# Gated delta rule on one NeuronCore: making the raw k kᵀ and k qᵀ products once per chunk pair and keeping them for both directions

## The chip, the core and the metric

The kernel runs on one NeuronCore of a Trainium2 chip. The metric is the device time of one execution in microseconds. Shown are three runs of the kernel before and one further execution recorded by the hardware profiler.

## What is computed

Two transformer blocks of width 1024 over 512 tokens, in fp32. The change lies in the first block, in its bidirectional gated delta rule: 8 heads of dimension 128, run once in increasing and once in decreasing position. The part of the reference that matters:

```python
def gated_delta_rule(q, k, v, g, beta):
    ...
    g = jnp.cumsum(g, axis=-1)
    decay = jnp.exp(jnp.where(tri_incl, g[..., :, None] - g[..., None, :], -jnp.inf))
    k_beta = k * beta[..., None]
    lower = jnp.where(tri_strict, jnp.einsum('bhncd,bhnsd->bhncs', k_beta, k) * decay, 0.0)
    rhs = jnp.concatenate([v * beta[..., None], k_beta * jnp.exp(g)[..., None]], axis=-1)
    sol = lax.linalg.triangular_solve(lower, rhs, left_side=True, lower=True, unit_diagonal=True)
    u, w = sol[..., :dv], sol[..., dv:]
    qk = jnp.einsum('bhncd,bhnsd->bhncs', q, k) * decay
    def step(state, xs):
        qd, kt, ui, wi, qki, gl = xs
        v_new = ui - jnp.einsum('bhck,bhkv->bhcv', wi, state)
        o = jnp.einsum('bhck,bhkv->bhcv', qd, state) + jnp.einsum('bhcs,bhsv->bhcv', qki, v_new)
        state = state * jnp.exp(gl)[..., None, None] + jnp.einsum('bhck,bhcv->bhkv', kt, v_new)
        return state, o

o_fwd = gated_delta_rule(q, k, v, g[:, :, 0], beta[:, :, 0])
o_bwd = rev(gated_delta_rule(rev(q), rev(k), rev(v), rev(g[:, :, 1]), rev(beta[:, :, 1])))
```

The products k kᵀ (the gram) and k qᵀ hold neither decay nor beta: these come in afterwards, element by element, and are what differs between the directions.

## The kernel before, in words

**Rounds.** The kernel cuts the 512 tokens into NC = 4 chunks of 128. The delta rule runs in eight rounds R = 0 to 7; `half = R // 4` picks four heads, `r = R % 4` the step of the scan. A round holds J = 8 problems: the four heads in the forward direction on chunk r (j = 0 to 3) and the same heads in the backward direction on chunk 3 − r (j = 4 to 7). So rounds r and 3 − r of a half use the same two chunks, with the directions exchanged. All of it lies in `delta(R)`, which each engine has for itself; semaphores join the four.

**The head of a round**, in the order of its data:
- TensorE (PE) spreads the cumulated decays into pA (L918), makes the eight grams k kᵀ into pB (L925, semaphore `gram`), runs a piece of a filler, waits for `eg` and makes the eight k qᵀ into pA (L933, semaphore `kq`), then runs a second piece of filler.
- VectorE (DVE) subtracts decays from pA into `et` (L2108), derives `en` (L2113) and masks `et` (L2117). ScalarE (ACT) takes the exponents: `qd` from pA (L1504, semaphore `eg`), `en` (L1506), `et` (L1508).
- DVE multiplies the grams in pB by beta and by `en`, eight instructions of 128x128 (L2124, semaphore `L`). ACT copies the diagonal blocks to `lc` (L1515, L1516). GpSimd (POOL) masks `lc` for each of six levels into `ls` (L2528). PE starts level 0 from the first `ls` (L902).
- DVE makes `tb` (L2133) and `ub` (L2135) from level 0; PE needs `ub` for level 1. At levels 1 and 2 DVE multiplies k qᵀ, still in pA, by `et`, 128x512 at a time (L2157).

**Fillers.** Between the steps of a round PE runs dense products of 128x512 (L641) of other projections, cut by the tables `GAP` and `GAP3`: in rounds 0 to 5 there are 14 products between L925 and L933 and 14 more before level 0, in rounds 6 and 7 there are 16 and 17. Each product has a weight tile that ACT (w_hi, L1210) and DVE (w_lo, L1788) have split. DVE has filler of its own, the taps of a 31-wide convolution (L1868), placed by the table `TAP`: three of them come between L2124 and L2133 in rounds 0 to 4, then more at each level. In round 7 the filler of PE is the product of the convolution's result; it waits for each slice k of `a_lo`, of which POOL makes slices 0 to 5 (L2561) and DVE slices 6 and 7 (L1847), in its order behind L2124.

The order on each engine is that of the program text; nothing is moved by a scheduler.

```python
dve.wait_ge(S("gram"), R + 1)
dve.wait_ge(S("en"), R + 1)
...
ins = dve.scalar_tensor_tensor(en[:, j], pB[:, j], scal(6, j), en[:, j], ALU.mult, ALU.mult)
...
if R == 7:
    for t in range(6, KT):
        low("conv", t, cslot(t))
```

Of the kernel before, what the change touches and what calls it, by code (L numbers as in the profile page):

```python
# [17 lines left out]
ALU = mybir.AluOpType  # L18
# [101 lines left out]
def build(nc, a, out):  # L120

    ctx = ExitStack()
    with ctx:
# [23 lines left out]
        w_lo = at("w_lo", 2 * UC, F32R, shape=[P, 2, UC])  # L147
        A_OFF = base[0]
# [43 lines left out]
        J = 2 * HH  # L192
        en = at("en", J * P, shape=[P, J, P])
# [429 lines left out]
        def _(pe):  # L623
# [282 lines left out]
            def delta(R):  # L906
# [15 lines left out]
                for j, d, hh, c in prob:  # L922

                    tok = slice(c * P, (c + 1) * P)
                    ins = pe.matmul(pB[:, j, :], kT[:, hh, tok], kT[:, hh, tok], start=True, stop=True)  # L925
                ins.then_inc(S("gram"), 1)
# [3 lines left out]
                pe.wait_ge(S("eg"), R + 1)  # L930
                for j, d, hh, c in prob:
                    tok = slice(c * P, (c + 1) * P)
                    ins = pe.matmul(pA[:, j, :], kT[:, hh, tok], qT[:, hh, tok], start=True, stop=True)  # L933
                ins.then_inc(S("kq"), 1)
                gap(R, 1)
                for lv in range(LEVELS):

                    pe.wait_ge(S("ls"), LEVELS * R + lv + 1)
                    if lv == 0:
# [4 lines left out]
                        if R == 5:  # L944

                            pe.wait_ge(S("csum"), KT - 1)
                            pe.matmul(nb, ones, acc[:], start=True, stop=True).then_inc(S("mean"), 1)
# [18 lines left out]
                    pe.wait_ge(S("ycp"), LEVELS * R + lv)  # L966
                    wait(pe, "t_upd", (LEVELS - 1) * R + lv - 1)
# [235 lines left out]
        def _(act):  # L1203
# [63 lines left out]
            def high_o(h):  # L1267
                act.wait_ge(S("on_z" if h < HH else "on_g"), h + 1)
                if h < HH:
                    act.wait_ge(S("kq"), 8)  # L1270
                    act.wait_ge(S("qdm"), 8)
                act.activation(o_hi[:, h], oT[:, h], ACT.Copy).then_inc(S("a_hi"), 1)
# [215 lines left out]
            def delta(R):  # L1488
# [27 lines left out]
                act.activation(lc[hi_], en[hi_, :, hi_], ACT.Copy).then_inc(S("lc"), 1)  # L1516
                gap(R, 0)
                gap(R, 1)
# [264 lines left out]
        def _(dve):  # L1783
# [309 lines left out]
            def delta(R):  # L2093
# [26 lines left out]
                dve.wait_ge(S("gram"), R + 1)  # L2120
                dve.wait_ge(S("en"), R + 1)
                dve.wait_ge(S("kf"), 3 * (half + 1))
                for j in range(J):
                    ins = dve.scalar_tensor_tensor(en[:, j], pB[:, j], scal(6, j), en[:, j], ALU.mult, ALU.mult)  # L2124
                ins.then_inc(S("L"), 1)
                if R == 7:
# [9 lines left out]
                for lv in range(1, LEVELS):  # L2136
# [15 lines left out]
                    if lv in (1, 2):  # L2152

                        dve.wait_ge(S("kq"), R + 1)
# [517 lines left out]
```

## Time and profile before

| | |
|---|---|
| three runs | 2248.22, 2248.62, 2251.39 us; median 2248.62 us |
| profiled execution, own time | 2249.63 us |
| its span in the trace | 2247.8 us |
| PE busy | 2181.4 us, 97% of the span |
| VectorE / ScalarE / GpSimd busy | 1274.1 us (57%) / 820.4 us (36%) / 196.0 us (9%) |
| chain that ended last | PE 80%, issue 10%, VectorE 7%, ScalarE 2% |

The delta rounds lie from about 217 to 430 us (R = 0 to 3) and from 530 to 752 us (R = 4 to 7). A PE matmul's end is modelled in the profile, so that neighbouring matmuls overlap by a little: what a group of matmuls takes from PE is read from its start to the start of what follows. An fp32 matmul of the program is two rows in the trace (x16 for eight). A number in square brackets is the time that the engine idled before the row, and for whom.

### The profile page before, as it was taken

The page shows a single profiled execution, that of the slowest core. Times are in us where ns is not written, and L with a number is a line of the kernel's source. Part 1 is how long each engine was busy: PE and PEld are TensorE (multiplying, and loading weights), DVE is VectorE, ACT ScalarE, POOL GpSimd, SP SyncE. Part 2 cuts the span into 40 slices and gives each one's busy share as a digit, 9 for nine tenths or more (in the row PEclk, how much of TensorE's full clock was granted, in tenths as well). Part 3 has the DMA queues.
Part 4 walks back from the last instruction along what each step waited for, and adds up shares of the span by engine and source line. Part 5 has one row for each costly group of instructions (what it writes and reads, how often), then busy time and mean ns, then how long its engine had stood idle before and what let it go on. Part 6 is the DMA issues. An engine that isn't in the chain of part 4 may idle for free.

```text
span 2247.8 us, 34856 instructions
## 1 busy us (share of the span) xinstructions
PE 2181.4 (97%) x14232; PEld 1819.0 (81%) x14232; DVE 1274.1 (57%) x1889; ACT 820.4 (36%) x1256; POOL 196.0 (9%) x142
## 2 busy tenths in 40 slices
PE   7999999998999999999999999999999899999998
PEld 5878788787888888888888888888897588888887
DVE  4789999887765555444532554443237736444423
ACT  4344434345444233232222532322233534232222
POOL 0100222102333001000000100000000110000000
PEclk9999999999999999999999989999999889999999
DMA  4232111121111243332332323333321112322321
GB/s 160 78 131 78 56 44 44 57 72 57 35 49 63 99 140 118 102 94 93 114 103 66 120 66 97 99 93 112 102 67 57 38 57 67 102 94 93 116 96 51
DMA packets 56171, 189.88 MB, mean 84 GB/s; under 512 B 6257, under 2 KB 8689, under 8 KB 56049
## 3 DMA queue, kind: packets, MB, share of 16 engines
q1 hardware_dynamic: 53168, 182.88, 25.3%
q10 hardware_dynamic: 2880, 5.24, 0.6%
q8 instruction: 92, 1.51, 0.3%
q14 instruction: 31, 0.25, 0.0%
HBM read 178.66 MB, written 9.44 MB: 84 GB/s over the span
## 4 chain that ended last, share of the span: by engine, by line
PE 80%; issue 10%; DVE 7%; ACT 2%; POOL 0%; DMA 0%; SPq 0%; ACTq 0%; DVEq 0%; POOLq 0%
PE pg L641 68%; PE pC L902 4%; PE pB L902 1%; DVE cpad L1868 1%; DVE w_lo L1788 1%; DVE sacc L2009 1%; PE pB L672 1%; ACT w_hi L1210 1%; PE pA L962 1%; PE pC L745 1%; PE pA L719 0%; PE pB L679 0%; PE pB L703 0%; PE pC L719 0%; PE pC L1170 0%
## 5 line engine op out<-in xcount | busy, mean ns | idle before, releaser
L641 PE MATMUL pg<-a_hi,w_hi 128*128 128x512 f32 (+1 forms) x1920 | 748.9, 390 | 12.4 <-DVE a_lo L1847 3.4
L641 PE MATMUL pg<-a_lo,w_hi 128*128 128x512 f32 (+1 forms) x1920 | 741.1, 386 | 0.0
L641 PE MATMUL pg<-a_hi,w_lo 128*128 128x512 f32 (+1 forms) x1920 | 738.6, 385 | 0.0
L1788 DVE TENSOR_TENSOR w_lo<-w_raw,w_hi 128x1024 fp32r<-128x1024 f32 (+3 forms) x299 | 382.6, 1279 | 399.2 <-ACT w_hi L1210 396.8
L1210 ACT ACTIVATE w_hi<-w_raw 128x1024 fp32r<-128x1024 f32 (+3 forms) x299 | 329.6, 1102 | 651.7 <-PE pg L641 640.7
L641 PEld LDWEIGHTS pg<-a_hi,w_hi 128*128 128x128 f32 x1920 | 364.0, 190 | 87.6 <-issue 8.0
L641 PEld LDWEIGHTS pg<-a_hi,w_lo 128*128 128x128 f32 x1920 | 363.6, 189 | 69.1 <-issue 1.6
L641 PEld LDWEIGHTS pg<-a_lo,w_hi 128*128 128x128 f32 x1920 | 363.8, 190 | 68.0 <-issue 0.9
L641 PE MATMUL pg<-h_hi,w_hi 128*128 128x512 f32 (+1 forms) x572 | 215.7, 377 | 0.6 <-DVE w_lo L1788 0.6
L641 PE MATMUL pg<-h_hi,w_lo 128*128 128x512 f32 (+1 forms) x572 | 214.5, 375 | 0.0
L641 PE MATMUL pg<-h_lo,w_hi 128*128 128x512 f32 (+1 forms) x572 | 212.4, 371 | 0.0
L2274 DVE TENSOR_TENSOR tmp<-pg,rstd 128x512 f32<-128x512 f32 x66 | 45.6, 691 | 188.6 <-PE pg L641 188.6
L1868 DVE SCALAR_TENSOR_TENSOR cpad<-cpad,vec 128x512 f32<-128x512 f32 x180 | 144.0, 857 | 0.3
L641 PEld LDWEIGHTS pg<-h_hi,w_lo 128*128 128x128 f32 x572 | 107.4, 188 | 21.3
L641 PEld LDWEIGHTS pg<-h_lo,w_hi 128*128 128x128 f32 x572 | 107.3, 188 | 20.4
L641 PEld LDWEIGHTS pg<-h_hi,w_hi 128*128 128x128 f32 x572 | 107.5, 188 | 19.2 <-DVE w_lo L1788 1.0
L2528 POOL TENSOR_TENSOR ls<-lc,consts 128x512 f32<-128x512 f32 x48 | 74.2, 1557 | 467.8 <-ACT lc L1516 422.1
L2575 POOL TENSOR_TENSOR acc<-acc,sq 128x512 f32<-128x512 f32 x22 | 29.7, 1349 | 819.3 <-ACT sq L1253 819.3
L1597 ACT ACTIVATE h_hi<-tmp 128x512 f32 (+1 forms) x66 | 41.7, 632 | 131.7 <-DVE tmp L2278 131.7
L2516 POOL TENSOR_TENSOR acc<-acc,sq 128x512 f32<-128x512 f32 x22 | 30.5, 1388 | 570.8 <-ACT sq L1227 570.5
L2283 DVE TENSOR_TENSOR h_lo<-tmp,h_hi 128x512 f32 (+1 forms) x66 | 45.7, 693 | 58.3 <-ACT h_hi L1597 58.3
L2269 DVE TENSOR_TENSOR tmp<-pg,rstd 128x512 f32<-128x512 f32 x66 | 45.6, 691 | 55.0 <-PE pg L641 54.9
(361 smaller groups left out, 2376.4 us busy)
## 6 DMA issues: line engine op xcount, KB each, us to landing
w_raw<-in_w_gu SPq DMA_DIRECT2D x132, 512.0 KB, 3.5
w_raw<-in_w_in SPq DMA_DIRECT2D x74, 512.0 KB, 3.5
w_raw<-in_w_dn SPq DMA_DIRECT2D x48, 704.0 KB, 4.1
spill_g<-tmp ACTq DMA_DIRECT2D x16, 256.0 KB, 2.1
w_raw<-in_w_co SPq DMA_DIRECT2D x8, 512.0 KB, 3.6
w_raw<-in_w_do SPq DMA_DIRECT2D x8, 512.0 KB, 3.6
w_raw<-in_w_wo SPq DMA_DIRECT2D x8, 512.0 KB, 4.1
w_raw<-in_w_pg SPq DMA_DIRECT2D x8, 512.0 KB, 3.5
```

The source lines that it names most:

```text
L641: ins = pe.matmul(dst[:, cols], w_of(w, n % 2, k), b(k)[:, cols], start=first and q == 0, stop=last and q == len(todo) - 1)
L902: ins = pe.matmul(dst[s, j, :], lhs[s, j, :], id64[s, :] if rhs is None else rhs[s, j, :], start=True, stop=True)
L1210: act.activation(w_hi[:, n % 2, 0:c], w_raw[:, n % 4, 0:c], ACT.Copy).then_inc(S("w_hi"), 1)
L1597: act.activation(h_hi[:, m] if isinstance(i, int) else h_hi[:, bass.ds(m, 1)].rearrange("p a n -> p (a n)"), tmp2[:], ACT.Copy).then_inc(S ...
L1788: dve.tensor_tensor(w_lo[:, n % 2, 0:c], w_raw[:, n % 4, 0:c], w_hi[:, n % 2, 0:c].bitcast(F32), ALU.subtract).then_inc(S("w_lo"), 1)
L1868: ins = dve.scalar_tensor_tensor(y, src, w, y, ALU.mult, ALU.add)
L2269: dve.tensor_tensor(tmp1[:], bg, rstd[:], ALU.mult).then_inc(S("evD"), 1)
L2274: dve.tensor_tensor(tmp2[:], bu, rstd[:], ALU.mult).then_inc(S("evD"), 1)
L2283: dve.tensor_tensor(at_m(h_lo), tmp2[:], at_m(h_hi).bitcast(F32), ALU.subtract)\
L2516: pool.tensor_tensor(acc[:], acc[:], sq[:, t % 2, :], ALU.add).then_inc(S("add"), 1)
L2528: pool.tensor_tensor(ls[:, lv % 2].rearrange("p (d h) c -> p d h c", d=2), lc[:].rearrange("p (d h) c -> p d h c", d=2), mask, ALU.mult)\
L2575: pool.tensor_tensor(acc[:], acc[:], sq[:, t % 2, :], ALU.add).then_inc(S("add"), 1)
```

## The change

The raw grams are made in rounds 0, 1, 4 and 5 only, and the raw k qᵀ in rounds 0, 1, 4, 5 and 6. Behind `lc`, ACT copies the grams of these four rounds, and the k qᵀ of rounds 0, 1 and 4, out of PSUM, as two instructions of 128x512 each (14 in all). They go into columns of the weight buffers that no weight of 1024 columns fills, and for round 1 into two unused tiles of oT. In rounds 2, 3, 6 and 7 DVE reads the gram from the copy of the twin round (3 − r), directions exchanged. In rounds 2, 3 and 7 it also reads k qᵀ there, and multiplies it right behind the grams' eight instructions rather than at levels 1 and 2. In round 5 a single matmul for a mean (into pB) moves from level 0 to level 1, behind ACT's `yb` copy. The diff, cut to its core:

```diff
+        spare = at("spare", 8 * UC, offset=first, shape=[P, 8, UC])
+        GRAM, KQ = (0, 1, 4, 5), (0, 1, 4, 5, 6)
+        def kept(what, R, d):
+            half, r = divmod(R, NC)
+            i = 4 * r + 2 * what + d
+            if i < 4:
+                return spare[:, 2 * i:2 * i + 2, KT * P:KT * P + 2 * P].rearrange("p a (b c) -> p a b c", c=P)
+            if i < 6:
+                s = 4 * (i - 4)
+                return spare[:, s:s + 4, KT * P + 2 * P:UC].rearrange("p (a b) c -> p a b c", b=2)
+            return oT[:, HH + i - 6].rearrange("p (a b c) -> p a b c", b=2, c=P)
+        def twin(R):
+            return R + NC - 1 - 2 * (R % NC)
+        def rounds(which, R):
+            return sum(z <= R for z in which)
 # PE, delta(R)
-                for j, d, hh, c in prob:
-                    tok = slice(c * P, (c + 1) * P)
-                    ins = pe.matmul(pB[:, j, :], kT[:, hh, tok], kT[:, hh, tok], start=True, stop=True)
-                ins.then_inc(S("gram"), 1)
+                if R in GRAM:
+                    for j, d, hh, c in prob:
+                        tok = slice(c * P, (c + 1) * P)
+                        ins = pe.matmul(pB[:, j, :], kT[:, hh, tok], kT[:, hh, tok], start=True, stop=True)
+                    ins.then_inc(S("gram"), 1)
                 gap(R, 0)
-                pe.wait_ge(S("eg"), R + 1)
-                for j, d, hh, c in prob:
-                    tok = slice(c * P, (c + 1) * P)
-                    ins = pe.matmul(pA[:, j, :], kT[:, hh, tok], qT[:, hh, tok], start=True, stop=True)
-                ins.then_inc(S("kq"), 1)
+                if R in KQ:
+                    pe.wait_ge(S("eg"), R + 1)
+                    for j, d, hh, c in prob:
+                        tok = slice(c * P, (c + 1) * P)
+                        ins = pe.matmul(pA[:, j, :], kT[:, hh, tok], qT[:, hh, tok], start=True, stop=True)
+                    ins.then_inc(S("kq"), 1)
-                        if R == 5:
-                            pe.wait_ge(S("csum"), KT - 1)
-                            pe.matmul(nb, ones, acc[:], start=True, stop=True).then_inc(S("mean"), 1)
                     pe.wait_ge(S("ycp"), LEVELS * R + lv)
+                    if R == 5 and lv == 1:
+                        pe.wait_ge(S("csum"), KT - 1)
+                        pe.matmul(nb, ones, acc[:], start=True, stop=True).then_inc(S("mean"), 1)
 # ACT, delta(R)
                 act.activation(lc[hi_], en[hi_, :, hi_], ACT.Copy).then_inc(S("lc"), 1)
+                if r < 2:
+                    for d in range(2):
+                        act.activation(kept(0, R, d), quarter(pB[:, d * HH:d * HH + HH]), ACT.Copy)
                 gap(R, 0)
+                if r < 2 and twin(R) not in KQ:
+                    act.wait_ge(S("kq"), rounds(KQ, R))
+                    for d in range(2):
+                        act.activation(kept(1, R, d), quarter(pA[:, d * HH:d * HH + HH]), ACT.Copy)
 # DVE, delta(R)
-                dve.wait_ge(S("gram"), R + 1)
+                dve.wait_ge(S("gram"), rounds(GRAM, R))
                 for j in range(J):
-                    ins = dve.scalar_tensor_tensor(en[:, j], pB[:, j], scal(6, j), en[:, j], ALU.mult, ALU.mult)
+                    d, hh = divmod(j, HH)
+                    g = pB[:, j] if R in GRAM else kept(0, twin(R), 1 - d)[:, hh // 2, hh % 2]
+                    ins = dve.scalar_tensor_tensor(en[:, j], g, scal(6, j), en[:, j], ALU.mult, ALU.mult)
                 ins.then_inc(S("L"), 1)
+                if R not in KQ:
+                    dve.wait_ge(S("et"), R + 1)
+                    for d in range(2):
+                        z = quarter(et[:, d * HH:d * HH + HH])
+                        dve.tensor_tensor(z, kept(1, twin(R), 1 - d), z, ALU.mult).then_inc(S("qk"), 1)
-                    if lv in (1, 2):
-                        dve.wait_ge(S("kq"), R + 1)
+                    if lv in (1, 2) and R in KQ:
+                        dve.wait_ge(S("kq"), rounds(KQ, R))
```

How it moves instructions, at three places. PE at the head of round 2, before (L1012 ends round 1; the L641 rows are the first filler products):

```order
L1012 MATMUL pC<-bv,kt 128x128 x8
L918 MATMUL pA<-consts,gat 128x128 x8
L925 MATMUL pB<-kT 128x128 x8
L641 MATMUL pg<-a_hi,w_hi 128x512
L641 MATMUL pg<-a_lo,w_hi 128x512
L641 MATMUL pg<-a_hi,w_lo 128x512
```

and now:

```order
L1039 MATMUL pC<-bv,kt 128x128 x8
L943 MATMUL pA<-consts,gat 128x128 x8
L666 MATMUL pg<-a_hi,w_hi 128x512
L666 MATMUL pg<-a_lo,w_hi 128x512
L666 MATMUL pg<-a_hi,w_lo 128x512
```

The filler now follows the decay spread directly; 14 products later the eight k qᵀ matmuls are gone too, so that 28 products stand in a row before level 0.

DVE at the head of round 2, before:

```order
L2193 SCALAR_TENSOR_TENSOR st<-st,gat,pC 128x128 x8
L1788 TENSOR_TENSOR w_lo<-w_raw,w_hi 128x1024
L2108 TENSOR_TENSOR et<-pA,gat 128x512 x2
L2113 TENSOR_SCALAR en<-et 128x1024
L2117 SCALAR_TENSOR_TENSOR et<-et,consts 128x512 x2
L2124 SCALAR_TENSOR_TENSOR en<-pB,gat,en 128x128 x8
L1868 SCALAR_TENSOR_TENSOR cpad<-cpad,vec 128x512 x3
L2133 TENSOR_TENSOR tb<-consts,ls 128x512
L2135 TENSOR_TENSOR ub<-consts,pC 128x512
```

and now (in round 2 the kept k qᵀ lies in oT, in round 3 in spare):

```order
L2234 SCALAR_TENSOR_TENSOR st<-st,gat,pC 128x128 x8
L1822 TENSOR_TENSOR w_lo<-w_raw,w_hi 128x1024
L2142 TENSOR_TENSOR et<-pA,gat 128x512 x2
L2147 TENSOR_SCALAR en<-et 128x1024
L2151 SCALAR_TENSOR_TENSOR et<-et,consts 128x512 x2
L2160 SCALAR_TENSOR_TENSOR en<-spare,gat,en 128x128 x8
L2166 TENSOR_TENSOR et<-oT,et 128x512 x2
L1902 SCALAR_TENSOR_TENSOR cpad<-cpad,vec 128x512 x3
L2174 TENSOR_TENSOR tb<-consts,ls 128x512
L2176 TENSOR_TENSOR ub<-consts,pC 128x512
```

Two multiplications of 128x512 now stand ahead of the three taps and of `tb`; they left levels 1 and 2.

DVE at the head of round 7, before and now (L1847 and L1881 make slices 6 and 7 of `a_lo`):

```order
L2117 SCALAR_TENSOR_TENSOR et<-et,consts 128x512 x2
L2124 SCALAR_TENSOR_TENSOR en<-pB,gat,en 128x128 x8
L1847 TENSOR_TENSOR a_lo<-cpad,a_hi 128x512 x2
L2133 TENSOR_TENSOR tb<-consts,ls 128x512
L2135 TENSOR_TENSOR ub<-consts,pC 128x512
```

```order
L2151 SCALAR_TENSOR_TENSOR et<-et,consts 128x512 x2
L2160 SCALAR_TENSOR_TENSOR en<-spare,gat,en 128x128 x8
L2166 TENSOR_TENSOR et<-spare,et 128x512 x2
L1881 TENSOR_TENSOR a_lo<-cpad,a_hi 128x512 x2
L2174 TENSOR_TENSOR tb<-consts,ls 128x512
L2176 TENSOR_TENSOR ub<-consts,pC 128x512
```

Here the same two multiplications stand ahead of the two slices of `a_lo`.

## Rows read from the trace of the kernel before

**Rows 1.** The page, part 1: busy time of each engine.
```profile
PE 2181.4 (97%) x14232; PEld 1819.0 (81%) x14232; DVE 1274.1 (57%) x1889; ACT 820.4 (36%) x1256; POOL 196.0 (9%) x142
```
**Rows 2.** Timeline, PE, head of round 2: start, us, engine, line, operation, idle before.
```profile
327.29 1.95 PE L925 MATMUL pB<-kT 128*128 128x128 f32 x16
328.99 0.48 PE L641 MATMUL pg<-a_hi,w_hi 128*128 128x512 f32 x1
...
337.65 1.15 PE L902 MATMUL pC<-consts,ls 64*64 64x64 f32 x32 [0.23 <-POOL ls L2528]
```
**Rows 3.** Timeline, the other engines, the same stretch, to PE's level 1.
```profile
325.70 2.16 DVE L2193 SCALAR_TENSOR_TENSOR st<-st,gat,pC 128x128 f32<-128x128 f32 x8 [0.50 <-PE pC L1012]
...
327.78 1.22 DVE L1788 TENSOR_TENSOR w_lo<-w_raw,w_hi 128x1024 fp32r<-128x1024 f32 x1
...
331.15 1.05 ACT L1506 ACTIVATE en<-en 128x1024 f32<-128x1024 f32 x1
...
332.30 2.16 DVE L2124 SCALAR_TENSOR_TENSOR en<-pB,gat,en 128x128 f32<-128x128 f32 x8
...
334.38 2.07 DVE L1868 SCALAR_TENSOR_TENSOR cpad<-cpad,vec 128x512 f32<-128x512 f32 x3
...
335.85 2.98 POOL L2528 TENSOR_TENSOR ls<-lc,consts 128x512 f32<-128x512 f32 x2 [36.93 <-ACT lc L1516]
...
337.62 1.75 DVE L2133 TENSOR_TENSOR tb<-consts,ls 128x512 f32<-128x512 f32 x1 [1.18 <-POOL ls L2528]
...
340.11 1.15 PE L902 MATMUL pC<-ub,ls 64*64 64x64 f32 x32 [0.66 <-DVE ub L2135]
```
**Rows 4.** Timeline, round 2, level 1: POOL and DVE at the same time.
```profile
345.13 2.95 POOL L2528 TENSOR_TENSOR ls<-lc,consts 128x512 f32<-128x512 f32 x2
345.43 3.87 DVE L1868 SCALAR_TENSOR_TENSOR cpad<-cpad,vec 128x512 f32<-128x512 f32 x3
```
**Rows 5.** Groups by line and shape: DVE on 128x128 out of SBUF alone.
```profile
L2454 DVE TENSOR_SCALAR sm<-sm,sml 128x128 f32<-128x128 f32 x8 | 1.9, 283 | 0.1
```
**Rows 6.** Timeline, head of round 7, DVE, PE and POOL.
```profile
702.30 2.15 DVE L2124 SCALAR_TENSOR_TENSOR en<-pB,gat,en 128x128 f32<-128x128 f32 x8
...
704.37 1.28 DVE L1847 TENSOR_TENSOR a_lo<-cpad,a_hi 128x512 fp32r<-128x512 f32 x2
...
705.10 0.50 PE L641 MATMUL pg<-a_hi,w_hi 128*128 128x512 f32 x1 [1.07 <-DVE a_lo L1847]
...
705.83 2.54 POOL L2528 TENSOR_TENSOR ls<-lc,consts 128x512 f32<-128x512 f32 x2 [4.60 <-ACT lc L1516]
...
708.76 1.15 PE L902 MATMUL pC<-consts,ls 64*64 64x64 f32 x32
```
**Rows 7.** Timeline, head of round 6: the first two levels' masks, and PE's level 0.
```profile
645.27 2.53 POOL L2528 TENSOR_TENSOR ls<-lc,consts 128x512 f32<-128x512 f32 x2 [17.06 <-ACT lc L1516]
...
647.30 1.15 PE L902 MATMUL pC<-consts,ls 64*64 64x64 f32 x32
```
**Rows 8.** Timeline, round 0: an ACT copy out of PSUM, and ACT before level 1.
```profile
218.73 0.58 ACT L1362 ACTIVATE ktok<-pC 128x512 f32<-128x512 f32 x1
...
236.44 0.60 ACT L1521 ACTIVATE yb<-pC 128x512 f32<-128x512 f32 x1 [2.51 <-PE pC L902]
```
**Rows 9.** Timeline, round 5: the mean's matmul.
```profile
594.53 1.13 PE L947 MATMUL pB<-acc,consts 128*128 128x512 f32 x2
```
**Rows 10.** Waits of PE over the whole span: total us, times, longest.
```profile
PE pB L1157 <- DVE sm L2454: 7.5, 5, 3.0
PE pB L679 <- DVE oT L1987: 6.6, 1, 6.6
```
**Rows 11.** Windows, PE: length, busy (instructions), granted clock, DMA share, GB/s.
```profile
759.00:767.00 8.00, 8.00 (x30) 0.57 0.31 98
521.00:523.00 2.00, 0.00 (x0) 0.50 0.00 0
1788.00:1792.00 4.00, 4.00 (x22) 0.50 0.35 122
```

More of the change, by code:

```diff
@@ L192, in build, with quarter @@
         J = 2 * HH
+        GRAM, KQ = (0, 1, 4, 5), (0, 1, 4, 5, 6)
[8 more added lines that the diff above has]
+            return oT[:, HH + i - 6].rearrange("p (a b c) -> p a b c", b=2, c=P)
+        def quarter(z):
+            return z.rearrange("p (a b) c -> p a b c", b=2)
+        def twin(R):
+            return R + NC - 1 - 2 * (R % NC)
+        def rounds(which, R):
+            return sum(z <= R for z in which)
         en = at("en", J * P, shape=[P, J, P])
@@ L1269, in high_o @@
                 if h < HH:
-                    act.wait_ge(S("kq"), 8)
+                    act.wait_ge(S("kq"), len(KQ))
                     act.wait_ge(S("qdm"), 8)
```

## The prediction

> **What bounds the kernel now.** I read the page's busy shares first, then the timeline at the head of each delta round, then the waits of PE and its granted clock. By the page, PE is the bound: busy for 97% of the span, against 57% for VectorE [rows 1]. If that held everywhere, every matmul taken away would be time gained. The share is an average, though, and the change takes matmuls from one place only, the head of a round, so that place decides.
>
> At the head of round 2 the reader should follow two threads from the end of round 1 to level 0. PE's thread is the decay spread, the grams, 14 products, k qᵀ and 14 products; it arrives at level 0 and finds the first mask `ls` 0.23 us late [rows 2]. The other thread is DVE, ACT and POOL. It starts when L1012 lets DVE update `st` at 325.70 and goes on with hardly a pause: `st`, then w_lo, then the subtractions and masks, the gram products from 332.30 to 334.46, ACT's `lc`, and POOL's masks from 335.85 [rows 3]. Nowhere on it does anything wait for the gram: the gram products start at 332.30 because ACT's exponent of `en` ends at 332.20 [rows 3], while the grams were done at 329 [rows 2]. So both threads take the same 12 us, and PE's is merely as long. Round 3 shows the same 0.23 us. PE is busy there, but level 0 is set by VectorE's thread.
>
> **What is taken from PE.** From the start of the grams at 327.29 to the first product at 328.99 is 1.70 us [rows 2]. Seven such groups go (four of grams, three of k qᵀ): 7 x 1.70 = 11.9 us of PE work. What each is worth depends on what PE then meets.
>
> **Rounds 2 and 3, the wait for `ls`.** PE loses 3.4 us of work and reaches level 0 at about 334.0 instead of 337.4. The mask still lands at 337.6. All 6.8 us of the two rounds turn into waits of about 3.6 us each: gain nothing.
>
> **Rounds 2 and 3, the moved multiplications.** They now stand behind the gram products and ahead of the three taps and `tb`. No row has them with both inputs in SBUF at this place. Their price lies between nothing (they fill DVE's idle 1.18 us before `tb` [rows 3]) and what they push into POOL's time. Three taps take 2.07 us alone [rows 3] but 3.87 us beside two masks, which in turn go from 2.53 us [rows 7] to 2.95 us [rows 4]: the two engines take turns, instruction by instruction. `tb` too takes 1.75 us beside a mask against a tap's 0.69 us [rows 3]. Following the turns: gram products end at 334.46, two multiplications at a tap's pace end at 335.8, tap 1 at 336.4, mask 0 at 337.6, tap 2 at 338.15, mask 1 at 339.25, tap 3 at 339.8, `tb` at 340.4, `ub` at 341.1. PE's level 1 starts at 341.2 instead of 340.11 [rows 3], and PE already waits for `ub` there today. That is +1.1 us; I give back 0.3 us because the taps of level 1 then start one multiplication sooner and DVE's next `ub` is less late. So +0.8 us a round, +1.6 us for both, between bounds of 0 and +2.2.
>
> The Trainium skill, page "SBUF — State Buffer", section "Who interferes with whom", says that a VectorE instruction with two SBUF inputs and a GpSimd instruction that reads SBUF exclude each other for whole instructions, while one input in PSUM avoids it. The trace agrees: 1.75 us for `tb` with two SBUF inputs. The change moves an input of k qᵀ's product from PSUM to SBUF, so the rule speaks against it; without the turns the sum would be the 0.2 us a round of the second rival below.
>
> **Round 7, the wait for `a_lo`.** PE loses 3.4 us of work here too, but already waits 1.07 us in the second filler piece for slice 6 of `a_lo`, which DVE makes behind the gram products [rows 6]. The two multiplications come ahead of it. Gram products end at 704.45, multiplications at 705.75, slice 6 at 706.4; then mask 0 (due at 705.83 [rows 6]) has its turn until 707.5, and slice 7 lands at 708.05. The 12 products that follow slice 7 take 2.85 us today (slice 7 at 705.65, level 0 at 708.76 with the last waits [rows 6]). Level 0 comes at about 711.0 instead of 708.76: +2.2 us. Without turns slice 7 lands 1.3 us later than now: +1.3 us. I take +2.2, since the turns are what rows 4 show.
>
> **Round 6, the one place with slack.** Only the grams go. Mask 0 ends at half of 2.53 us after 645.27, at 646.5, and PE starts level 0 at 647.30 without a wait [rows 7]. With 0.3 us from mask to PE, as in round 2, 0.5 of the 1.70 us is gained: −0.5 us.
>
> **Rounds 0, 1, 4, 5.** The copies: 14 of 0.58 us [rows 8]. In round 0 four of them take 2.3 us, and ACT idles 2.51 us before level 1's copy [rows 8]; rounds 1 and 4 have as much idle time in two pieces, round 5 has two copies and more. Cost 0; if that cover were gone, 0.2 to 0.4 us a round on PE's wait for `yb`. The mean's matmul, 1.13 us [rows 9], leaves a place where it covered part of PE's wait for `ub` for one where PE goes without a wait: +0.45 us, between 0 and +1.1.
>
> **A price unseen.** The gram products read SBUF instead of PSUM in four rounds. They take 2.16/8 = 0.27 us each now [rows 3]; the nearest instruction out of SBUF alone takes 1.9/8 = 0.24 us [rows 5]. Bounds: −0.03 x 8 x 4 = −1.0 us and 0. I take 0, as the arithmetic per element is the same.
>
> Sum of the terms: 1.6 + 2.2 − 0.5 + 0.45 = **+3.75 us**, with 11.9 us of PE work gone.
>
> **The clock.** Waits of about 3.6 us (rounds 2 and 3, with another of some 1.7 us one step later) and of 4 us and more (round 7, today's 1.07 + 3.4 + 0.6 and more for slice 7) are new. In the trace, PE's wait of 6.6 us and the attention's wait of 3.0 us [rows 10] come with a granted clock of 0.50 during or behind them, that is 1.2 instead of 2.4 GHz [rows 11]; once the kernel is under way I found no wait of this length without. At half clock PE's work takes double. In rounds 2 and 3 a part of such a stretch passes while PE waits anyway; I estimate 1.1 us each, and 2 us in round 7: +4.2 us, bounds 0 and, if each of three stretches were all PE work, 3 x 3.4 = +10.2 us (a mean of 0.57 over 8 us [rows 11] is 8 x 0.43 x 2 = 6.9 us at half clock, of which half is lost). The Trainium skill, page "TensorE: Matmul & The Clock Gate", section "HAM oscillation — how this bites in real kernels", describes the same: pauses inside a kernel bring the low clock back each time. By that rule alone all three waits cost; without it the time would be the first rival's.
>
> Forecast: 3.75 + 4.2 = +8.0 us. Against the profiled execution's 2249.63 us that is 2257.6; this execution is 1.0 us above the median of the runs, 2248.62, which gives **2256.6 us**. A measurement of this kernel can tell about 0.2%, 4.5 us, from no change.
>
> **The rivals.**
> - *Waits, but no low clock*: +3.75 us, 2252.4 us. For it: none of the shorter waits of today's rounds, up to 1.2 us, lowers the clock. Against: rows 10 and 11. Chance 0.20; a third of it lies above 4.5 us.
> - *Waits without turns*: DVE's moved work fits beside POOL's, rounds 2 and 3 cost 0.2 us each, round 7 +1.3: 0.4 + 1.3 + 0.45 − 0.5 = +1.65, 2250.3 us. Chance 0.15. Against: rows 4.
> - *Low clock at full price*: 3.75 + 10.2 = +14, 2262.6 us. Chance 0.12.
> - *Faster, PE is the bound after all*: if the mask and slice 7 land early enough, every group counts: −11.9 + 0.45 = −11.5 us, 2237.1 us. Its place is level 0 of rounds 2, 3 and 7; it decides where `ls` comes 3.4 us ahead of PE, that is where DVE's thread shortens by that much. For it: 97% busy [rows 1], and waits for `ls` of only 0.23 us today. Against: 0.23 us of wait means no slack at all, and nothing on the thread is taken out. Chance 0.06. A part of it, −2 to −6 us (quicker gram products, more slack in round 6 than I read), has 0.05.
>
> That the matmuls are not really dropped is excluded by the order of instructions.
>
> **How the numbers follow.** My forecast has 0.42. Slower by over 0.2%: 0.42 + 0.12 + a third of 0.20 = 0.60. Faster by over 0.2%: 0.06 and most of the 0.05, 0.10. Within: 0.30. The range runs from 2246 (the no-clock and no-turn cases, the −1.0 us of the unseen price and half of the small gains) to 2263 (the full price of the clock); outside are the fast case, part of the small gains and the tail above, together under 0.2.
>
> **What would show it.** In the new profile: matmuls L950/L958 in four and five rounds only; PE's wait for POOL's `ls` in rounds 2 and 3 grown from 0.23 to about 3.6 us each; the wait for `ub` at level 1 from 0.66 to 1.5 or more; PE's wait for `a_lo` in round 7 from 1.07 to over 4 us; granted clock under 1.00 at these places, where it is 1.00 now; ACT's copies in time that was idle. I am wrong if PE starts level 0 of rounds 2 and 3 clearly less than 11.9 us after L1012's end, or if the clock holds at 1.00 through waits of 3.6 us.

## The result, and the profile after

The change is slower: its runs have a median of 2255.5 us, those of the kernel before beside them 2247.6 us, a ratio of 1.0049 (95% interval 1.0036 to 1.0062), some 8 to 14 us; the two medians by themselves lie 7.9 us apart. The forecast was 2256.6 us. A second series of the same kernel gave 1.0028 (1.0017 to 1.0039), so the size that can be stated is 4 to 14 us; what is known of the difference between two series of one kernel is said at the end. PE's busy time fell a little; nothing else in the first line of the page explains a slower kernel (compare [rows 1]):

```profile
PE 2178.0 (96%) x14120; PEld 1813.9 (80%) x14120; DVE 1270.7 (56%) x1889; ACT 827.9 (37%) x1270; POOL 197.9 (9%) x142
```

PE has 112 matmuls less in that line (56 of fp32, two rows each) and should be 11.9 us less busy; it is 3.4 us less. The windows below show where much of the rest has come back: as matmuls at half clock. PE's waits over the whole span (total us, times, longest); before, the same three come to 1.5 us, 3.4 us and 2.8 us:

```profile
PE pC L927 <- POOL ls L2569: 8.4, 3, 3.7
...
PE pg L666 <- DVE a_lo L1881: 5.9, 5, 4.1
PE pC L927 <- DVE ub L2176: 3.8, 6, 1.7
```

The timeline of the change at the head of round 2, all engines (start in us, duration in us, engine, line, operation; idle before in brackets), with the same steps as [rows 2, 3]:

```profile
326.37 1.95 PE L943 MATMUL pA<-consts,gat 128*128 128x128 f32 x16
...
333.17 2.20 DVE L2160 SCALAR_TENSOR_TENSOR en<-spare,gat,en 128x128 f32<-128x128 f32 x8
335.28 1.29 DVE L2166 TENSOR_TENSOR et<-oT,et 128x512 f32<-128x512 f32 x2
336.49 4.11 DVE L1902 SCALAR_TENSOR_TENSOR cpad<-cpad,vec 128x512 f32<-128x512 f32 x3
336.75 3.30 POOL L2569 TENSOR_TENSOR ls<-lc,consts 128x512 f32<-128x512 f32 x2 [36.95 <-ACT lc L1543]
...
338.41 1.15 PE L927 MATMUL pC<-consts,ls 64*64 64x64 f32 x32 [3.69 <-POOL ls L2569]
...
341.12 0.67 DVE L2176 TENSOR_TENSOR ub<-consts,pC 128x512 f32<-128x512 f32 x1
341.94 1.98 PE L927 MATMUL pC<-ub,ls 64*64 64x64 f32 x32 [1.66 <-DVE ub L2176]
```

From the decay spread to level 0 it is 338.41 − 326.37 = 12.04 us, as before (12.15). PE's missing 3.4 us stand there as a wait of 3.69. From level 0 to level 1 it is 3.53 us instead of 2.46, since `ub` comes behind the multiplications and the taps (L2166, L1902); and the 32 small matmuls of level 1 take 1.98 us instead of 1.15, at half clock. Round 3 does the same with a wait of 3.71. The next view has PE of the change behind the wait of round 2, in stretches of 2 us (length, busy (instructions), granted clock, DMA share, GB/s); 1.00 is the full clock:

```profile
339.00:341.00 2.00, 1.28 (x22) 0.75 0.23 92
341.00:343.00 2.00, 1.06 (x20) 0.50 0.10 39
343.00:345.00 2.00, 2.00 (x21) 0.50 0.32 102
345.00:347.00 2.00, 2.00 (x34) 0.54 0.45 172
347.00:349.00 2.00, 2.00 (x45) 1.00 0.00 0
...
395.67:405.00 9.33, 8.93 (x115) 0.51 0.27 87
...
713.00:720.00 7.00, 6.89 (x34) 0.58 0.00 0
```

The last two lines are from rounds 3 and 7. The kernel before has the full clock in all three places; its PE in the same view:

```profile
341.00:348.00 7.00, 7.00 (x148) 1.00 0.27 88
395.00:405.00 10.00, 9.92 (x214) 1.00 0.25 76
709.00:716.00 7.00, 7.00 (x139) 1.00 0.01 2
```

Round 7 in the change, the timeline that answers to [rows 6]:

```profile
711.17 1.28 DVE L2166 TENSOR_TENSOR et<-spare,et 128x512 f32<-128x512 f32 x2
712.37 1.28 DVE L1881 TENSOR_TENSOR a_lo<-cpad,a_hi 128x512 fp32r<-128x512 f32 x2
712.62 3.40 POOL L2569 TENSOR_TENSOR ls<-lc,consts 128x512 f32<-128x512 f32 x2 [4.63 <-ACT lc L1543]
713.11 0.80 PE L666 MATMUL pg<-a_hi,w_hi 128*128 128x512 f32 x1 [4.08 <-DVE a_lo L1881]
714.55 0.63 PE L666 MATMUL pg<-a_hi,w_hi 128*128 128x512 f32 x1
714.98 0.63 PE L666 MATMUL pg<-a_lo,w_hi 128*128 128x512 f32 x1
...
719.42 1.15 PE L927 MATMUL pC<-consts,ls 64*64 64x64 f32 x32
```

PE waits 4.08 us for slice 6 of `a_lo` instead of 1.07, and then makes a product each 0.43 us (714.98 − 714.55), where 0.23 is normal.

**Where the 9.8 us went.** The time of a round is read from the start of its decay spread (L918, L943) to that of the next, since every kernel here has the same work between these two points. Round 3 is followed by some 90 us of other work, and its column ends where PE begins its wait of 6.6 us [rows 10]; round 7 ends at its level 0. The last column has everything between its two points, the stretch behind that cut too. Rounds 0, 1 and 4 are left out of the table: they agree within 0.06 us in all kernels, but for round 4 of the ninth. Microseconds:

| | round 2 | round 3 | round 5 | round 6 | head of 7 | round 0 to level 0 of 7 |
|---|---|---|---|---|---|---|
| before | 54.35 | 137.63 | 52.81 | 60.04 | 14.39 | 491.3 |
| change | 57.26 | 140.85 | 53.15 | 59.38 | 18.30 | 501.1 |
| difference | +2.91 | +3.22 | +0.34 | −0.66 | +3.91 | +9.8 |

From there to the end the change has 1537.6 us and the kernel before 1539.0: in this pair of executions the loss lies in the rounds.

### The profile page after: what moved, and what is told of

Its sections match the earlier page's. It is cut to its first block, busy times and chain, and to the rows that moved or that the text cites. A ratio compares the mean times of both kernels' runs of the same rounds, so it can differ in the third digit from the quotient of the medians.

```text
span 2257.0 us, 34640 instructions
## 1 busy us (share of the span) xinstructions
PE 2178.0 (96%) x14120; PEld 1813.9 (80%) x14120; DVE 1270.7 (56%) x1889; ACT 827.9 (37%) x1270; POOL 197.9 (9%) x142
## 4 chain that ended last, share of the span: by engine, by line
PE 81%; DVE 9%; issue 7%; ACT 2%; DMA 0%; POOL 0%; SPq 0%; DVEq 0%; ACTq 0%; POOLq 0%
PE pg L666 69%; PE pC L927 4%; DVE cpad L1902 2%; PE pB L927 1%; DVE w_lo L1822 1%; PE pB L697 1%; DVE sacc L2043 1%; ACT w_hi L1237 1%; PE pC L770 1%; PE pA L985 1%; PE pA L744 0%; PE pB L704 0%; PE pB L1025 0%; PE pA L1033 0%; PE pB L728 0%
## 5 line engine op out<-in xcount | busy, mean ns | idle before, releaser
L1902 DVE SCALAR_TENSOR_TENSOR cpad<-cpad,vec 128x512 f32<-128x512 f32 x180 | 142.4, 850 | 0.3
```

The lines of the kernel that those rows point to most:

```text
L1902: ins = dve.scalar_tensor_tensor(y, src, w, y, ALU.mult, ALU.add)
```

## The experiments

Line numbers past 927 differ by up to ten from kernel to kernel, as the text above them grows. Every sum that is called "the rounds" is the last column of the table above. Ratios are to the kernel before.

**1. Only the multiplications back.** Copies kept, PE work dropped, but k qᵀ of rounds 2, 3 and 7 multiplied at levels 1 and 2 again, from the copy:

```diff
-                if R not in KQ:
-                    dve.wait_ge(S("et"), R + 1)
-                    for d in range(2):
-                        z = quarter(et[:, d * HH:d * HH + HH])
-                        dve.tensor_tensor(z, kept(1, twin(R), 1 - d), z, ALU.mult).then_inc(S("qk"), 1)
...
+                    if lv in (1, 2) and R not in KQ:
+                        dve.wait_ge(S("et"), R + 1)
+                        z = quarter(et[:, (lv - 1) * HH:lv * HH])
+                        dve.tensor_tensor(z, kept(1, twin(R), 2 - lv), z, ALU.mult).then_inc(S("qk"), 1)
```

> The change, with the two multiplications of k q' put back to levels 1 and 2 of rounds 2, 3 and 7 (they still read the kept copies). Theory (moved multiplications push the taps into POOL's time and slices 6 and 7 of a_lo back): PE's wait for ub at level 1 of round 2 falls from 1.66 us to about 0.7, level 1 starts 2.5 us after level 0 as in the kernel before and not 3.5; the wait for slice 6 of a_lo falls from 4.1 to about 2.8 us and level 0 of round 7 comes 1.3 to 2.2 us sooner; the 3.7 us waits for ls stay, and so do the low clocks. About 3 to 4 us less than the change. Rival (the multiplications' place costs nothing, all of it is the clock): within 1 us of the change, waits for ub and a_lo as in the change.

Measured: 2245.0 us, ratio 0.9995 (0.9981 to 1.0010); the rounds 495.5 us, 4.2 above before and 5.6 below the change. PE's waits in rounds 2 and 3, and in round 7:

```profile
PE pC L927 <- POOL ls L2568: 7.6, 2, 3.8
...
PE pg L666 <- DVE a_lo L1881: 2.9, 1, 2.9
```

The step from level 0 to level 1 is 2.46 us again in round 3, as in the kernel before, though the clock falls within it (0.73 from 396 to 397 us, then 0.50); in round 2, where all of it runs at half clock, it is 3.05 us. PE has no wait for `ub` there, as the slower work ahead of level 1 covers it. So the extra microsecond of that step came from the multiplications; experiment 2 shows the same at full clock. The wait for `ls` stays at 3.8 us and the low clock goes with it in both rounds (in round 2 a granted clock of 0.66 between 338 and 348 us): rounds 2 and 3 are still 1.53 and 0.68 us longer than before, round 7's head 1.63 us. Dropping PE's work alone costs time in these rounds.

**2. PE's work back, everything else as in the change.** The grams and k qᵀ of rounds 2, 3 and 7 are made again, and nobody reads them:

```diff
+                elif R in (2, 3, 7):
+                    for j, d, hh, c in prob:
+                        tok = slice(c * P, (c + 1) * P)
+                        pe.matmul(pB[:, j, :], kT[:, hh, tok], kT[:, hh, tok], start=True, stop=True)
...
+                elif R in (2, 3, 7):
+                    pe.wait_ge(S("eg"), R + 1)
+                    for j, d, hh, c in prob:
+                        tok = slice(c * P, (c + 1) * P)
+                        pe.matmul(pA[:, j, :], kT[:, hh, tok], qT[:, hh, tok], start=True, stop=True)
```

> The change, but PE makes the grams and k q' of rounds 2, 3 and 7 all the same, and nobody reads them. Adds 10 us of PE work to the change. Theory (level 0 is set by DVE's thread, and the low clock comes from the long waits): PE's waits for ls shrink from 3.7 to about 0.2 us, level 0 comes no later, the granted clock in rounds 2 and 3 is 1.00 again, and the kernel is 3 to 4 us FASTER than the change (2 us a round in rounds 2 and 3; round 7 still waits about 2.4 us for a_lo and may keep its low clock). Rival (PE is the bound): 10 us slower than the change. Rival (waits, but their clock costs nothing): the same as the change within 1 us.

Measured: 2247.7 us, ratio 1.0016 (0.9999 to 1.0033); the rounds 495.2 us. With 6 x 1.70 = 10.2 us more PE work than the change, its rounds are 5.9 us shorter. This is the run that decides: in the change, PE's work at these places has a negative price. It is the rounds that show it; the interval of the ratio overlaps that of the change's second series, 1.0017 to 1.0039. PE's waits in rounds 2 and 3 together, with none for `ls` left, and in round 7:

```profile
PE pC L927 <- DVE ub L2185: 3.4, 2, 1.7
...
PE pg L666 <- DVE a_lo L1890: 2.3, 1, 2.3
```

And PE's windows (the columns as above), in round 2 from level 1 on, and in round 3 from level 0 on:

```profile
341.00:348.00 7.00, 5.29 (x90) 0.76 0.35 116
...
396.02:405.00 8.98, 7.27 (x155) 1.00 0.25 90
```

Round 3 keeps the full clock and is 0.75 us longer than before: that is the price of the moved multiplications by itself. Round 7 keeps it too, at +1.25 us. Round 2 has the same wait of 1.71 us at the same step, yet a low clock behind it, and is 2.29 us longer.

**3. The copies and the mean's matmul alone.**

```diff
-        GRAM, KQ = (0, 1, 4, 5), (0, 1, 4, 5, 6)
+        GRAM, KQ = tuple(range(8)), tuple(range(8))
...
-                if r < 2 and twin(R) not in KQ:
+                if R in (0, 1, 4):
```

> The kernel before, with only the 14 ACT copies added (nobody reads them) and the mean's matmul moved to level 1 of round 5. Theory: the copies lie in ACT's idle time; every round but 5 keeps its length within 0.1 us, round 5 grows by 0.3 to 0.5 us from the mean. Total 0 to +1 us against before. Rival (the copies delay w_hi or level 1's yb): rounds 0, 1 and 4 grow by 0.2 to 0.4 us or more each.

Measured: 2242.5 us, ratio 0.9984 (0.9964 to 1.0004). Every round is within 0.04 us of the kernel before but round 5, +0.34 us, where the matmul for the mean moved. The 14 copies cost nothing that shows. They take idle time: in round 0 of the change ACT idles 0.44 us ahead of level 1's copy (timeline, ACT), where it idled 2.51 us in [rows 8]:

```profile
237.33 0.60 ACT L1555 ACTIVATE yb<-pC 128x512 f32<-128x512 f32 x1 [0.44 <-PE pC L927]
```

**4. The gram's half of the change.** k qᵀ is made in all eight rounds; the grams only in four:

```diff
-        GRAM, KQ = (0, 1, 4, 5), (0, 1, 4, 5, 6)
+        GRAM, KQ = (0, 1, 4, 5), tuple(range(8))
```

> The change with the grams dropped in rounds 2, 3, 6 and 7, but k q' made in every round and multiplied at levels 1 and 2. Theory: level 0 of rounds 2 and 3 comes no sooner, PE waits for ls 0.23 + 1.7 = 1.9 us there, partly before k q' (it waits for eg); waits of under 2 us leave the clock at 1.00, so rounds 2 and 3 keep their length of before, round 6 gains 0.6 us, round 7 stays as before (its wait for a_lo grows from 1.1 to 2.8 us; if the clock falls there, +2 us). Total -0.3 to +2 against before. Rival (PE is the bound): four groups of 1.7 us gained, -6.8 us.

Measured: 2248.1 us, ratio 1.0015 (0.9997 to 1.0033). Rounds 2 and 3 and the head of round 7 are as before to 0.01 us; round 6 is 0.62 us shorter; the rest is round 5's matmul. Of 4 x 1.70 = 6.8 us of PE work, 6.2 became waits. PE's waits in rounds 2 and 3, and its clock in round 2:

```profile
PE pC L927 <- POOL ls L2569: 2.2, 2, 1.1
...
341.00:348.00 7.00, 7.00 (x149) 1.00 0.27 78
```

The lengths of rounds 2 and 3 show that all of their 3.4 us went into waits: 1.7 us more for `ls` and 1.3 us ahead of k qᵀ, for ACT's `qd`, are named in the trace. Behind the wait of 1.1 us at level 0 the clock stays at 1.00 here.

**5. The mask sooner, on the change.** To test that the mask's thread sets level 0, the `w_lo` that DVE makes at the head of rounds 2 and 3, for a weight of the last filler piece of the round ahead, goes behind the gram products:

```diff
                         for key in filled(R, q):
-                            after(key)
+                            if last and R + 1 in (2, 3):
+                                later.append(key)
+                            else:
+                                after(key)
...
                 ins.then_inc(S("L"), 1)
+                while later:
+                    after(later.pop(0))
```

> The change, with one instruction of DVE moved in rounds 2 and 3: w_lo (1.22 us), which stands ahead of the subtraction of the decays, goes behind the gram products. Theory (DVE's thread sets level 0, not PE): the masks land about 1.2 us sooner, PE's waits for ls fall from 3.7 to about 2.5 us or are partly replaced by a wait for this w_lo, and from the decay spread to level 0 are 10.9 us instead of 12.04. Rival (something else gates the head, such as PE's fillers or POOL): still 12.0 us.

Measured, one run: 2252.8 us; the rounds 498.9 us. From decay spread to level 0 it is 11.37 us instead of 12.04: the thread moved it, with PE's work unchanged, by half of what the shift of 1.2 us allowed. The timeline (the decay spread starts at 325.65 here, so mask 0 starts 9.24 us behind it instead of 10.38; but DVE runs `w_lo` and both multiplications, L2172, without a pause, and PE goes on 2.1 us after the mask started, instead of 1.7):

```profile
333.43 1.22 DVE L1822 TENSOR_TENSOR w_lo<-w_raw,w_hi 128x1024 fp32r<-128x1024 f32 x1
...
334.56 1.29 DVE L2172 TENSOR_TENSOR et<-oT,et 128x512 f32<-128x512 f32 x2
...
334.70 0.50 PE L666 MATMUL pg<-a_hi,w_hi 128*128 128x512 f32 x1 [1.64 <-DVE w_lo L1822]
334.89 3.76 POOL L2575 TENSOR_TENSOR ls<-lc,consts 128x512 f32<-128x512 f32 x2 [35.81 <-ACT lc L1543]
...
337.02 1.97 PE L927 MATMUL pC<-consts,ls 64*64 64x64 f32 x32 [1.13 <-POOL ls L2575]
```

Level 0 itself now ran at half clock (1.97 us): two waits, 1.64 and 1.13 us, with 1.2 us of products between them, were followed by the fall as one of 3.7 had been. Level 1 came 4.18 us behind level 0 instead of 3.53, and round 2 was no shorter (57.30 us). In round 3 the low clock lasted some 3 us, and that round was only 0.76 us longer than before.

**6. The same edit on the kernel before.**

> The kernel before, with the same w_lo moved behind the gram products in rounds 2 and 3. Theory (in the kernel before both threads are equally long): the wait for ls of 0.23 us goes, and since PE has no other slack the stretch from the decay spread to level 0 falls from 12.15 us by 0.2 to 0.3 us only, against 1.2 us with the same edit in the change. Rival (DVE alone sets the head): 1.2 us shorter here too.

Measured, one run: 2243.3 us. Decay spread to level 0 is 11.83 us instead of 12.15, the rounds 2 and 3 are 0.27 and 0.28 us shorter. In the kernel before as well the mask comes last, but only by the 0.23 us of [rows 2]: behind it PE's own thread stands.

**7. Filler from later levels into the hole.** Experiment 1, with k qᵀ made in round 7 again, and with the 28 products ahead of level 0 of rounds 2 and 3 made 40, taken from later levels:

```diff
-        GRAM, KQ = (0, 1, 4, 5), (0, 1, 4, 5, 6)
+        GRAM, KQ = (0, 1, 4, 5), (0, 1, 4, 5, 6, 7)
...
-            gaps = GAP3 if len(filler(R)) == 3 else GAP
+            gaps = [20, 20, 2, 3, 0, 3, 0, 1, 0, 3, 0, 3, 3, 4, 5, 5] if R in (2, 3) else GAP3 if len(filler(R)) == 3 else GAP
```

> A version meant to use what the change frees: multiplications back at levels 1 and 2, k q' made again in round 7, and in rounds 2 and 3 twelve filler products (3 each from behind levels 1 to 4, where PE comes 0.7 to 1 us after its operand is ready) moved to the head, 20 + 20 instead of 14 + 14. Theory: the wait for ls falls from 3.8 to about 1.1 us, no low clock in rounds 2 and 3, each of them 2.4 to 2.7 us shorter than in the kernel before, round 6 0.65 shorter, round 5 0.35 longer, round 7 as before: 5 to 6 us less than before over the eight rounds, ratio about 0.9975. Rival (the products behind the levels cover VectorE's work, which is busy for 50 of 54 us in these rounds): new waits for ub at levels 2 to 5 give most of it back, and the rounds keep 54 us.

**8. More of it**, 22 + 22 products:

```diff
+            gaps = [22, 22, 2, 3, 0, 3, 0, 1, 0, 3, 0, 3, 3, 3, 4, 3] if R in (2, 3) else GAP3 if len(filler(R)) == 3 else GAP
```

> As the one before, with four more products of rounds 2 and 3 moved to the head (22 + 22; one less behind level 5 and in the next step, two less behind the last step). Theory: the wait for ls falls to 0.2 us; another 0.5 us gained in each round if the last steps have slack, 0 if their waits for en and bv grow by the same. Rival: as above, new waits at the end of the round, longer than e7.

Measured: 2247.4 us, ratio 1.0004 (0.9990 to 1.0018), and 2247.1 us, 1.0009 (0.9996 to 1.0023); the rounds 490.2 and 493.5 us. Rounds 2 and 3 become 0.43 and 0.25 us shorter in the first, 2.03 and 0.65 us longer in the second. The hole at level 0 closes and opens at the later levels, where DVE makes `ub`. PE's waits in rounds 2 and 3, experiment 7:

```profile
PE pC L927 <- DVE ub L2176: 7.3, 6, 2.3
PE pC L927 <- POOL ls L2568: 2.2, 2, 1.1
```

and experiment 8:

```profile
PE pC L927 <- DVE ub L2176: 8.0, 4, 2.8
...
PE pC L927 <- POOL ls L2568: 0.4, 2, 0.2
```

The reason lies in DVE's window over round 2 of the kernel before (the same columns, DVE's busy time):

```profile
324.50:378.50 54.00, 49.99 (x85) 1.00 0.14 46
```

DVE is busy for 50 of 54 us. By the page it has 57% [rows 1], but in these rounds it is nearly as full as PE. Filler that leaves the later levels uncovers DVE's work there.

**9. Experiment 7, with DVE's taps moved out of rounds 2 and 3.** A table for these two rounds leaves out the three taps between level 1 and level 2's `ub`; round 4 takes them, six in all:

```diff
-        TAP4 = [1, 2, 0] + [1, 1] * 4 + [1, 2] + [0, 10, 0]
+        TAP4 = [1, 2, 0] + [1, 2] * 4 + [1, 3] + [0, 11, 0]
+        TAP23 = [1, 2, 0, 1, 0, 0, 2, 1, 3, 1, 2, 1, 3, 0, 10, 0]
...
-                    taps((TAP4 if R == 4 else TAP)[g])
+                    taps((TAP4 if R == 4 else TAP23 if R in (2, 3) else TAP)[g])
```

> The filler-to-head version (20 + 20 products in rounds 2 and 3), with VectorE relieved: the three convolution taps behind level 1 and before level 2's ub of rounds 2 and 3 go to round 4 (six taps in all). Theory (in rounds 2 and 3 VectorE is as full as PE, and those three taps in turns with POOL's masks make ub of level 2 late by 2.3 us): the 2.3 us wait for ub falls below 0.5 us, rounds 2 and 3 fall from 53.9 to about 52 us, round 4 grows by less than 1 us; 4 to 5 us less than before over the eight rounds, ratio about 0.998. Rival: round 4, whose VectorE has 44 us of work in 52, grows by what rounds 2 and 3 gain (3 to 4 us), or other waits for ub take its place; same as e7.

Measured: 2244.9 us, ratio 0.9997 (0.9985 to 1.0009); rounds 2 and 3 are 2.39 and 2.03 us shorter, round 4 is 4.07 us longer, and the rounds together 492.2 us. PE's waits in rounds 2 and 3, then from round 4 to 600 us:

```profile
PE pC L928 <- DVE ub L2177: 2.8, 4, 0.8
...
PE pC L928 <- DVE ub L2177: 2.2, 2, 1.2
```

In rounds 2 and 3 part of the removed PE time can be had once DVE is lighter, and round 4, where DVE's work goes, gives it back. No version here is measurably faster than the kernel before.

**10. The change again**, in one series with experiment 9, no edit.

> The change itself once more, on the same chip as the version above and its runs of before. Theory: waits for ls of 3.7 us in rounds 2 and 3 and 4.1 us for a_lo in round 7 again, each followed by granted clock 0.50; +9 to +11 us from round 0 to the end of round 7 against before, whatever the rest of the program does; ratio 1.002 to 1.006. Rival (the low clocks were that execution's accident): some of the three places at clock 1.00, rounds 2 and 3 shorter by 2 us each.

Measured: 2251.4 us, ratio 1.0028 (1.0017 to 1.0039); the rounds 500.8 us, against 501.1. The waits return within 0.02 us (timeline, PE, round 2, round 3, round 7):

```profile
336.04 1.41 PE L927 MATMUL pC<-consts,ls 64*64 64x64 f32 x32 [3.71 <-POOL ls L2569]
...
392.87 1.97 PE L927 MATMUL pC<-consts,ls 64*64 64x64 f32 x32 [3.70 <-POOL ls L2569]
...
711.03 0.79 PE L666 MATMUL pg<-a_hi,w_hi 128*128 128x512 f32 x1 [4.09 <-DVE a_lo L1881]
```

Each is followed by the low clock, as in the first series. The sums agree better than their parts: round 2 is 0.43 us shorter than in the first series and the head of round 7 0.55 us, round 5 is 1.02 us longer. The rest of the program differs by more (last section).

## Why the prediction was right

The sign, the place and the waits were right. Two terms were off in opposite directions, and the sum came closer than they did: +8.0 us forecast, +9.8 in the profiled pair. That the forecast time of 2256.6 us lies 1.1 us from the median is luck in part: it starts from a median 1.0 us above the one of all runs of the kernel before, and the two series put the change some 11 and 6 us above it. The differences are those of the table, and the splitting between multiplications and clock uses experiment 2, whose round 3 and round 7 show the first without the second.

| step of the forecast | forecast us | measured us |
|---|---|---|
| PE's work removed in rounds 2, 3, 7, without its clock | 0 | 0 (experiment 4: the grams' half) |
| moved multiplications, rounds 2 and 3 | +1.6 | +1.5 (2 x 0.75) |
| slices of `a_lo`, round 7 | +2.2 | +1.25 |
| low clock, rounds 2 and 3 | +2.2 | +4.6 (2.91 + 3.22 − 1.5) |
| low clock, round 7 | +2 | +2.7 (3.91 − 1.25) |
| round 6 | −0.5 | −0.66 |
| the mean's matmul, round 5 | +0.45 | +0.34 |
| the copies; grams from SBUF | 0; 0 | 0; 0 |
| sum | +8.0 | +9.8 |

The split of round 2 rests on round 3's 0.75, as round 2 of experiment 2 had a low clock of its own. The second series of the change would give +4.0 and +2.1 for the two clock terms.

- **PE's wait for `ls`**: forecast 3.6 us each, found 3.69 and 3.71. **For `ub`**: 1.5 us or more; 1.66 in round 2, but 0.40 in round 3, where level 0 itself ran at half clock and took up the time. **For `a_lo`**: over 4 us; 4.08. All three granted clocks fell. Experiment 5 moved level 0 of round 2 by moving only DVE's work, so the thread named in the forecast does set it.
- **"+2.2 us, since the turns are what rows 4 show"** is the first step that failed: the term stood at +2.2 and measured +1.25. In round 2 the two engines did take turns: three taps took 4.11 us, two masks 3.30. In round 7 they did not: two multiplications 1.28 us and two slices 1.28 us back to back, and it is the masks, 3.40 us for two, that waited. The bound "without turns" (+1.3) is what came (+1.25). A pattern read where tap and mask alternate does not carry to a run of short instructions of one engine. Here the Trainium skill (page "SBUF — State Buffer", section "Who interferes with whom") says that an instruction of VectorE with two inputs in SBUF contends with one of GpSimd that reads SBUF; the trace agrees, 3.40 us for two masks that take 2.53 alone [rows 7].
- **"I estimate 1.1 us each"** for the low clock is the second. The falls cost 2.3 us each in rounds 2 and 3. An estimate of 1.1 us stands for 2.2 us of PE's time at half clock; in round 3 PE worked 8.93 us at a mean of 0.51. Not all of that is lost: some takes the place of waits, as the one for `ub`, 1.71 us in experiment 2 and 0.40 us here. The other bound (3.4 each) was too high. The length of 8 us was read from the stretch 759 to 767 us [rows 11], which has no wait before it (last section). What the Trainium skill says on the page "TensorE: Matmul & The Clock Gate", section "HAM oscillation — how this bites in real kernels" (pauses inside a kernel bring the low clock back each time), held at all six long waits of the two series of the change, 3.69 to 4.09 us.
- **The unseen price**, gram products out of SBUF, was 0: 346 ns against 343. DVE's groups by line and shape in the change (busy us, mean ns, idle before):

```profile
L2160 DVE SCALAR_TENSOR_TENSOR en<-spare,gat,en 128x128 f32<-128x128 f32 x32 | 8.8, 346 | 0.1
L2160 DVE SCALAR_TENSOR_TENSOR en<-pB,gat,en 128x128 f32<-128x128 f32 x32 | 8.6, 343 | 2.5 <-issue 2.4
```

- **The rivals.** "PE is the bound after all" fell with experiments 1, 2 and 4: 6.8 us of PE work gave 0.6 us, all in the one place with slack. "Waits, but no low clock" fell at all three places of the change; only behind shorter waits, 1.71 us in round 3 and 2.3 us in round 7 of experiment 2, did the clock hold. "Waits without turns" was right in round 7 and wrong in rounds 2 and 3. "Low clock at full price" was too high, 10.2 us against 7.3.

Still open is why the same wait of 1.71 us (experiment 2) and the same of 2.8 us (experiment 8) were followed by the low clock in round 2 and not in round 3. As far as seen, the work around them is alike, and no run took it apart. A different order of DVE's work in round 7 wasn't tried.

## What to carry to other kernels

A busy share of 97% over a whole program doesn't say that a removed matmul is time gained: look, at the very place, for the wait that comes last, and for the second thread that is as long. Where PE and a chain over other engines are balanced, taking work from PE leaves a hole, and a hole can cost more than the time it takes, when TensorE's granted clock falls for the matmuls behind it: here 10 us of matmuls nobody reads made the rounds 5.9 us shorter. Before removed work is turned into time, something has to be taken off the other thread, and the engine that makes that thread (here VectorE, 50 of 54 us) needs room for it at this place, not on average.

## What the runs showed of the hardware that was not expected

**The same program has a remainder that varies by 10 us.** The change and its second series are one and the same kernel. In the two profiled executions the tail from one and the same matmul of round 7 (L1025, at 754.91 and at 752.29 us) to the end took 1502.1 and 1492.6 us. PE's windows over most of it, first the change and then the second series:

```profile
755.00:2240.00 1485.00, 1467.00 (x7037) 0.98 0.28 91
```

```profile
755.00:2240.00 1485.00, 1462.79 (x7082) 0.99 0.28 92
```

A mean clock lower by 0.01 over 1485 us stands for some 30 us more at half clock, of which half is lost; the two values are rounded, so 9.5 us fit. The kernel before had 1503.5 us at 0.98 in its tail.

In one place it can be seen that falls of the clock come or stay away from one execution to the next: the kernel before has a mean of 0.57 from 759 to 767 us [rows 11], with PE busy throughout and no wait of 0.3 us or more in the 6 us before. Eight of the twelve profiled executions have such a fall between 758 and 777 us, 4 to 8 us long; the second series of the change is one of the four that have none. From round 0 to level 0 of round 7 no execution has a fall without a wait: each stands behind, or begins in, a wait of 1.7 us or more, or the two shorter ones of experiment 5. What decides falls without a wait was not found.

The consequence is practical: experiment 1 has rounds 4.2 us longer than before and a median that can't be told from it. Totals don't resolve here what stages do: rounds 0 and 1 repeat to 0.06 us in all twelve executions. Not all stages are so steady. Round 5 took 53.15 us in the first series of the change and 54.17 in the second, where PE waits 0.96 us for `en` (L2185); experiments 6 and 9 have this wait too. And the stretch between the cut of round 3 and round 4 took 12.8 to 14.3 us, with a low clock of varying length around the wait of 6.6 us. So sums of the rounds are sure to 1 or 2 us only, which leaves the 9.8 and the 5.9 standing, but not the 1.1 us by which experiment 7 is below the kernel before.

**How long a fall lasts varies more than the wait ahead of it.** Each wait of 3.7 to 4.1 us, nine in all, came with one: six in the two series of the change, two in experiment 1, one in experiment 5. So did the one of 2.9 us in round 7 of experiment 1 (a granted clock of 0.76 from 709 to 716 us). Behind the same 4.1 us (4.08, 4.09 and 4.09) the head of round 7 took 18.30, 17.75 and, in experiment 5, 17.33 us. Waits of 1.7 us (experiment 2) and 2.8 us (experiment 8) were followed by the low clock in round 2 and not in round 3, one of 2.3 us (experiment 2, round 7) was not. The kernel before already had a fall behind a wait under 3 us, which the forecast doesn't list: behind PE's wait of 2.38 us that ends at 1732.65 us the granted clock is 0.50. In experiment 8, PE behind the wait of 2.82 us in round 2 and behind the 2.83 us in round 3:

```profile
352.00:354.00 2.00, 2.00 (x35) 0.58 0.57 219
...
408.00:410.00 2.00, 1.81 (x38) 1.00 0.61 236
```

The first fell, the second held. And behind two waits of 1.6 and 1.13 us, close together, the clock fell in both rounds of experiment 5; behind the one of 1.1 us of experiment 4 it had not.
